# A gated attention and expert layer: gate products one by one beside the first wave's attention, sigmoid at the merge

## The reference

```
n = rms_norm(x);  proj = n @ w_in      # fox q|k|v|forget, sb q|k|v, ga, gb (1024 columns each)
y_fox = fox_attention(...) @ w_o_fox;  y_sb = stick_breaking_attention(...) @ w_o_sb
merged = sigmoid(ga) * y_fox + sigmoid(gb) * y_sb
h = x + merged @ w_out
out = h + peer_ffn(rms_norm(h))        # 8 heads x 16 experts per row, each a row of expert_u and expert_v
```

## Time and profile before

| | us |
|---|---|
| median of 3 runs (3985.39 to 3996.05) | 3988.52 |
| the profiled execution | 3995.0 |
| its span | 3993.0 |
| first gate piece on TensorE (L889) | 158.9 |
| first gather of expert rows (L764) | 538.5 |
| first wave's gate read issued (L737) | 356.6 |

### The profile page before, as it was taken

How to read it: one execution, slowest core, us unless ns; L and a number is a source line. 1 busy time by engine, 2 the same in 40 slices (tenths; PEclk the granted TensorE clock), 3 DMA queues, 4 the chain that set the end, 5 groups by cost and what they waited for, 6 DMA issues and landing times.

```text
span 3993.0 us, 32329 instructions
## 1 busy us (share of the span) xinstructions
PE 3143.7 (79%) x9766; PEld 1628.7 (41%) x9766; DVE 2769.3 (69%) x5660; ACT 1196.2 (30%) x2585; POOL 1392.3 (35%) x1087
## 2 busy tenths in 40 slices
PE   8998957879888697868887779997587878767655
PEld 3344633334436243335445435553262333234222
DVE  2021388678758967767867988886888866567766
ACT  1242111146511111146621146662101444011110
POOL 0000014335323324424333334443334434434553
PEclk9978978878788888978888989988798878878787
DMA  4422269999999969988999989999999888999997
GB/s 157 140 77 107 95 247 381 405 382 412 369 427 379 380 236 406 409 333 354 359 382 380 393 329 403 398 374 368 404 404 398 345 342 356 415 408 384 414 423 323
DMA packets 296027, 1367.21 MB, mean 342 GB/s; under 512 B 36056, under 2 KB 96624, under 8 KB 149392
## 3 DMA queue, kind: packets, MB, share of 16 engines
q0 software_dynamic: 154464, 1116.02, 68.5%
q1 hardware_dynamic: 110480, 222.78, 15.3%
q10 hardware_dynamic: 30912, 26.35, 2.0%
HBM read 1329.52 MB, written 35.10 MB: 342 GB/s over the span
## 4 chain that ended last, share of the span: by engine, by line
PE 40%; DVE 22%; DMA 17%; ACT 8%; issue 6%; SPq 3%; ACTq 2%; POOL 1%; DVEq 0%; POOLq 0%
PE pv L861 12%; DMA uv<-expert_uv,rows_u 9%; DVE uv L1488 9%; PE pb L1049 6%; PE pb L990 5%; SPq L572 3%; DVE held L1511 3%; PE pb L843 3%; PE pb L963 3%; PE pb L814 3%; PE pb L938 3%; PE pv L889 2%; DMA arena<-scratch_c_p 2%; ACTq L97 1%; DMA arena<-scratch_gates 1%
## 5 line engine op out<-in xcount | busy, mean ns | idle before, releaser
L764 POOL DMA_INDIRECT uv<-expert_uv,rows_u x1024 | 1336.5, 1305 | 1994.8 <-PE pv L861 1169.7
L861 PE MATMUL pv<-uv,diag 128*128 128x512 f32 x2344 | 1253.8, 692 | 337.2 <-ACT diag L1193 261.7
L1488 DVE CUSTOM_DVE_ANT_0 uv<-uv,nr 128x1024 f32<-128x1024 f32 x1056 | 1241.9, 1220 | 214.5 <-DMA uv<-expert_uv,rows_u 181.6
L861 PEld LDWEIGHTS pv<-uv,diag 128*128 128x128 f32 x2344 | 508.8, 225 | 985.8 <-issue 906.8
L1049 PE MATMUL pb<-arena 128*128 128x512 f32 (+1 forms) x1248 | 566.4, 613 | 74.2 <-DVE arena L1636 53.1
L1511 DVE SCALAR_TENSOR_TENSOR held<-uv,wgt,held 128x1024 f32<-128x1024 f32 x470 | 604.1, 1285 | 16.9 <-DVE wgt L1499 0.5
L1200 ACT ACTIVATE gel<-dots 128x4 f32<-128x4 f32 x264 | 54.2, 205 | 1720.6 <-DVE dots L1488 1658.0
L1049 PEld LDWEIGHTS pb<-arena 128*128 128x128 f32 (+1 forms) x1248 | 235.7, 192 | 383.2 <-issue 344.4
L814 PE MATMUL pb<-arena 64*128 64x512 f32 (+4 forms) x480 | 227.5, 590 | 124.4 <-DMA arena<-scratch_c_p 46.6
L990 PE MATMUL pb<-arena 128*128 128x256 f32 (+1 forms) x1280 | 260.9, 363 | 2.2 <-ACT arena L1293 2.2
L990 PEld LDWEIGHTS pb<-arena 128*128 128x128 f32 x1280 | 227.9, 194 | 42.2 <-issue 12.9
(11 more groups left out here) (180 smaller groups left out, 2658.0 us busy)
## 6 DMA issues: line engine op xcount, KB each, us to landing
arena<-w_stream SPq DMA_DIRECT2D x80, 1024.0 KB, 9.2
arena<-w_main SPq DMA_DIRECT2D x60, 1024.0 KB, 11.5
uv<-expert_uv,rows_u POOLq DMA_INDIRECT x1024, 12.0
scratch_gates<-arena ACTq DMA_DIRECT2D x32, 256.0 KB, 8.7
arena<-scratch_gates SPq DMA_DIRECT2D x8, 1024.0 KB, 19.6
o<-x SPq DMA_DIRECT2D x14, 512.0 KB, 8.3
arena<-scratch_c_p SPq DMA_DIRECT2D x8, 520.0 KB, 13.2
arena<-x_t SPq DMA_DIRECT2D x8, 512.0 KB, 4.8
```

The costliest lines, as they stand in the source:

```text
L764: pool.indirect_dma_start(out=uv[k % NU][:].rearrange("p a n -> p (a n)"), out_offset=None, in_=io["expert_uv"][:, :], in_offset=bass.Indi ...
L861: mm = nc.tensor.matmul(pv[:, c * BANK:(c + 1) * BANK], diag[n % ND][:], uv[k % NU][:, 1, c * BANK:(c + 1) * BANK], start=n == first, stop ...
L1488: nc.vector.tensor_tensor_reduce(out=u, in0=u, in1=row[:], scale=1.0, scalar=0.0, op0=ALU.mult, op1=ALU.add, accum_out=dots[b % 2][:, k % ...
```

## The change

The gate pieces of the first wave are no longer made as wholes. `gate_run(i)` makes product i % 8 of piece i // 8. The three pieces ahead of the attention are 24 such products in a row, as before. The other nine are 72 products, two in each of the 36 steps from -2 to 33 (`runs_at`): one between the value products and the turns, one behind the scores. A piece so spreads over four steps, and the last one ends in step 33 (before: the block of step 30). ScalarE takes a piece one step after its last product (before: two steps after its block), and the last piece at the start of the merge.

The piece is stored without its sigmoid (`ACT.Copy` with the row's scale), so the two table loads around it are gone within the loop. In the merge of a wave whose first tile is 0 or 8, that is waves 0 and 4, ScalarE applies the sigmoid in place to the gates that were read back, one instruction of 2048 columns for each tile, behind the copies of the turned outputs, and VectorE's gate products wait for it (`gated`). Waves 1 to 3 stay as they are.

```diff
--- before.py
+++ after.py
@@ -294,10 +294,19 @@
     return GATES + j // ABREAST, j % ABREAST
 
 
-def piece_at(s):
-
-    j = ABREAST + (s + 2) // 4
-    return j if (s + 2) % 4 == 0 and j < PIECES else None
+RUNS = 2
+RUNS_OF_PIECE = KD
+
+
+def runs_at(s):
+
+    n = ABREAST * RUNS_OF_PIECE + (s + 2) * RUNS
+    return [i for i in range(n, n + RUNS) if ABREAST * RUNS_OF_PIECE <= i < PIECES * RUNS_OF_PIECE]
+
+
+def pieces_done_at(s):
+
+    return [i // RUNS_OF_PIECE for i in runs_at(s) if i % RUNS_OF_PIECE == RUNS_OF_PIECE - 1]
 
 
 def tile_of(k):
@@ -468,7 +477,7 @@
         turned, turned_out = sem("turned_b"), sem("turned_b_out")
         summed_up, o_out = sem("summed_up"), sem("o_out")
 
-        gates_in = [sem(f"gates_in{i}") for i in range(2)]
+        gates_in, gated = [sem(f"gates_in{i}") for i in range(2)], sem("gated")
         x_in = [sem(f"x_in_m{i}") for i in range(2)]
         g_in = sem("g_in")
         chunk_in = [sem(f"chunk_in{i}") for i in range(NW)]
@@ -876,35 +885,39 @@
                         if b:
                             background(b - 1)
 
-                def gates(j):
-
+                def gate_run(i):
+
+                    j, half, f = i // RUNS_OF_PIECE, i % RUNS_OF_PIECE // 4, i % 4
                     (c, ti), r = piece(j), rows_of(NEW[0][piece(j)[1]])
-                    if j >= 2:
+                    n = chunk_no(0, 2 * c + half)
+                    if j >= 2 and half == 0 and f == 0:
                         pe.wait_ge(staged, proj.staged[(0, *piece(j - 2))])
-                    for half in range(2):
-                        n = chunk_no(0, 2 * c + half)
+                    if f == 0:
                         pe.wait_ge(chunk_in[n % NW], 16 * (n // NW + 1))
-                        w = wring[n % NW].rearrange("p (k n) -> p k n", k=4)
-                        for f in range(4):
-                            mm = nc.tensor.matmul(pv[0:r, j % 2 * BANK:(j % 2 + 1) * BANK], x_turned(ti, half * 4 + f, r), w[:, f, :],
-                                                  start=half == 0 and f == 0, stop=half == 1 and f == 3)
-                        if half:
-                            mm.then_inc(proj_ready, 1)
-                        elif ti == ABREAST - 1:
-                            mm.then_inc(chunk_used, 1)
+                    mm = nc.tensor.matmul(pv[0:r, j % 2 * BANK:(j % 2 + 1) * BANK], x_turned(ti, half * 4 + f, r),
+                                          wring[n % NW].rearrange("p (k n) -> p k n", k=4)[:, f, :],
+                                          start=half == 0 and f == 0, stop=half == 1 and f == 3)
+                    if f == 3 and half:
+                        mm.then_inc(proj_ready, 1)
+                    elif f == 3 and ti == ABREAST - 1:
+                        mm.then_inc(chunk_used, 1)
 
                 def attend(g):
                     n0, units = plan.first[g], plan.end[g] - plan.first[g]
                     for s in range(-2, units + 2):
                         if 2 <= s:
                             values(n0 + s - 2)
+                        if not g:
+                            for i in runs_at(s)[0:1]:
+                                gate_run(i)
                         turns = len(plan.turns[n0 + s - 1]) if 0 < s <= units else 0
                         for i in range(turns):
                             turn(n0 + s - 1, i)
                         if s + 2 < units:
                             scores(n0 + s + 2)
-                        if not g and piece_at(s) is not None:
-                            gates(piece_at(s))
+                        if not g:
+                            for i in runs_at(s)[1:]:
+                                gate_run(i)
                         if 0 <= s < units:
                             beside(("attend", g, s))
 
@@ -1109,8 +1122,8 @@
                         pe.wait_ge(q_out, wave_heads(g))
                     if g == 0:
                         pe.wait_ge(sk_in, 32)
-                        for j in range(ABREAST):
-                            gates(j)
+                        for i in range(ABREAST * RUNS_OF_PIECE):
+                            gate_run(i)
                     if NEW[g]:
                         pe.wait_ge(staged, proj.all_staged[g] if g else proj.staged[0, GATES - 1, ABREAST - 1])
                         pe.wait_ge(col_turned_out, proj.all_turned[g])
@@ -1218,7 +1231,7 @@
                     if c - 2 in QK:
                         act.wait_ge(col_turned, proj.turned[0, c - 2, ti] + 1)
                     act.wait_ge(s_stored[slot], proj.s_stored[0, c - 2, ti])
-                    nc.scalar.activation(stage[slot][0:r], pv[0:r, j % 2 * BANK:(j % 2 + 1) * BANK], ACT.Sigmoid,
+                    nc.scalar.activation(stage[slot][0:r], pv[0:r, j % 2 * BANK:(j % 2 + 1) * BANK], ACT.Copy,
                                          scale=rstd[0:r, ti:ti + 1]).then_inc(staged, 1)
                     act.wait_ge(staged, proj.staged[0, c, ti])
                     act.dma_start(dram["gates"][first_row(t):first_row(t) + r, (c - GATES) * BANK:(c - GATES + 1) * BANK],
@@ -1249,9 +1262,9 @@
                             take_output(n0 + s - 2)
                         if s + 2 < units:
                             magnitudes(n0 + s + 2)
-                        if not g and piece_at(s - 2) is not None:
-                            take_gates(piece_at(s - 2))
-                            nc.scalar.preload_act_table_set("natural_log_exp_and_others")
+                        if not g:
+                            for j in pieces_done_at(s - 1):
+                                take_gates(j)
                         if inside:
                             behind(("attend", g, s))
                             if plan.lots.get(("attend", g, s), ()):
@@ -1260,6 +1273,15 @@
                 def merge(g):
                     tiles = plan.tiles[g]
                     width = sum(query_rows(t) for t in tiles)
+                    if not g:
+                        for j in pieces_done_at(plan.end[0] + 1):
+                            take_gates(j)
+
+                    def sigmoids():
+                        for ti, t in enumerate(tiles):
+                            r = query_rows(t)
+                            act.wait_ge(gates_in[ti], 16 * (g + 1))
+                            nc.scalar.activation(gate[ti][0:r], gate[ti][0:r], ACT.Sigmoid).then_inc(gated, 1)
 
                     def take_outputs():
                         for ti, t in enumerate(tiles):
@@ -1307,6 +1329,8 @@
                         behind(("merge", g, s), 0, early)
                         if step[0] == "outputs":
                             take_outputs()
+                            if tiles[0] in NEW[0]:
+                                sigmoids()
                         elif step[0] == "merged":
                             take_merged()
                         elif step[0] == "norm":
@@ -1656,7 +1680,10 @@
                         cols = slice(c * BANK, (c + 1) * BANK)
                         for ti, t in enumerate(tiles):
                             r = query_rows(t)
-                            dve.wait_ge(gates_in[ti], 16 * (g + 1))
+                            if tiles[0] in NEW[0]:
+                                dve.wait_ge(gated, NEW[0].index(t) + 1)
+                            else:
+                                dve.wait_ge(gates_in[ti], 16 * (g + 1))
                             dve.wait_ge(y_ready, 2 * tiles[0] + c * len(tiles) + ti + 1)
                             for k in range(KINDS):
                                 ins = nc.vector.tensor_tensor(gate[ti][0:r, k, cols], gate[ti][0:r, k, cols], pb[0:r, ti * 2 + k, :], ALU.mult)
```

## The result

The changed kernel takes 3936.7 us (median of 3 runs, 3931.7 to 3943.2) where the kernel before takes 3988.5: a ratio of 0.9868 with a 95% interval of 0.9836 to 0.9899, 52 us faster. The forecast was 3942. Timed again it gave 3938.4 and 0.9868 (0.9851 to 0.9885).

What follows compares the result with a forecast made beforehand. The first wave's unbroken chain of waits, through attention and merge, was taken to bound the time before gathers at 538 us. Attention 48 plus merge 2.5 less last tile 4 gave 46.5 us: 3942 against the median 3988.5, range 3926 to 3967.

Steps and rivals of the forecast that it cites:

- The period: First attention: four steps with eight gate products take 14.6 us plus hand-overs, instead of 20.3.
- hand-overs: First attention: 0.1 us added to each step.
- The round: First attention: scores' start through ScalarE to the next values, 1.3 us, just covered by TensorE's work behind the turns.
- The clock: First attention: TensorE's clock near 1.0 from 180 us to the merge, where it averaged 0.76.
- the rival on the other side: First attention: clock does not stay up; at 0.50 throughout 71 us slower, 4060 us; chance of slower 0.04.
- The tables: First attention: two loads of 1.28 us go from each of nine pieces, already gone from the sum.
- The merge: First wave's merge: turns and first output products at full clock save 2.5 us, both sigmoids hidden.
- The last tile: Wave 4's merge: the added sigmoid costs 4 us, between ends of 2 and 14.
- The rival of 10 us either way: From 700 us on: changed order of gathers and weights shifts the time to 3932 or 3952; taking 10 or more, 0.07.

Runs made afterwards that it cites:

- singles_both_in_front: Changed kernel with both gate products of a step between values and turns, none behind the scores: 3962.4 us, ratio 0.9925 to the kernel before.
- the first experiment: Kernel before with gate pieces kept as whole blocks but stored raw, their sigmoid taken at the merge: 3987.1 us, ratio 0.9999.
- blocks_raw_filled: Whole raw blocks as in the first experiment, plus 21 unread 512-column products in steps without a piece: 3966.5 us, 0.9943 to the kernel before.

## Why the prediction was right

*The period.* 14.6 us and 0.4 of hand-overs were put down; step 2 began at 190.04 us (forecast 190.2) and step 6 at 204.43, so 14.4. Without a piece of tile 8 the periods took 14.4 to 14.6, and the two with one 15.7 (204.43 to 220.12, and the one from 249.12). Step 30 began at 293.81 for 295.2 with its hand-overs, and the outputs were turned at 306.84 for 308. The way, from groups' starts at full clock, was sound. That it came so close is in part luck, for its terms miss in opposite directions: the mask, put at 0.2 us, takes 0.06 or 0.07 from its start to the next product's, a single gate product, put at 0.865, takes 0.91 to 0.96 (227.90 to 228.86, 230.00 to 230.92), no hand-overs show beyond this, and that the pieces of tile 8 are dearer was not foreseen. The round was just covered, and its 1.3 us were right; because of the mask what covers it was overrated, which is why both products in front cost 22 us and not 16 in singles_both_in_front.

*The clock.* It was the condition of the whole forecast, and it held at 1.00. In the kernel before, it fell behind two short steps (those of 245.80 and 248.16 us) and not three. Against the rival on the other side stood that full-width products fill part of every step; the fillers, which are just that, raised the clock of the whole blocks from 0.76 to 0.97.

*The tables.* Right in the sum, since it was made from TensorE's groups and not by adding up savings. But the account of causes that I held at the first experiment gave the loads and part of the clock 22 to 33 us by themselves; alone they gave 5.5 of the attention and nothing measurable in the time. What I had not seen is that removing a wait of ScalarE leaves the narrow short steps, after which the clock falls anyway.

*The merge.* 2.5 us were expected from turns and first output products at full clock, 1.7 came (from 49.6 to 51.3). All of it is in the turns and copies, 4.48 us for 6.17; the clock did not last into the output products (0.82 from 312 to 320 us), which took 29.4 us for 29.6. The gates landed at 317.2 and 319.6, 10.4 and 12.8 us behind P, the end of the attention, where 9 and 11.8 had been taken: the last piece's store took 4.6 us to land and not 1.9, and SyncE waited for it, so that the read was issued at 312.37, 2 us later than put down. The table load did not come on top because it ran before the wait, and a sigmoid took 1.91, not 2.06 us. The first tile's sigmoid was through at 319.11, and 4.6 us were to spare, not 2.5.

*The last tile.* 4 us were put down; the changed kernel lost 4.3 to 4.7 in the stage, while the end shows nothing in one pair of kernels and 8 us in another. If it is nothing there, this is the term that was mis-sized and 4 of the 5 us between the forecast and the result. But these 5 us are within the range of the three runs (3931.7 to 3943.2), and need no cause.

*The stream.* The rival of 10 us either way did not come, but a spread of some 10 us to either side in single profiles (3441.6 to 3461.2 us from the first gather to the end) was real and is why single runs can't settle the small terms.

## What to carry to other kernels

Before pricing a wait on a slow engine, look at TensorE's granted clock behind it: if it is low there, removing the wait alone may give nothing, since TensorE then sets the pace at half speed. Independent full-width products belong into every step of a latency-bound loop, behind the instruction whose result makes the round through the other engines, not in a block; where there are none, even products that nobody reads can pay. And a saving ahead of a stream was worth its full size at the end here, while small costs within a stream that fills the DMA engines may not show there at all.

## What was not expected of the hardware

Added work made a kernel faster: 21 products more, 20.6 us less. With both products in front TensorE idled up to 0.76 us in a step, more than the 0.59 us of a period of the raw blocks, and the clock stayed at 1.00 (98.9 of 112 us busy, the window below), while in the kernel of whole raw blocks it was 0.76 at 105.3 us busy: recorded busy time does not tell whether the clock holds.

```profile
188.00:300.00 112.00, 98.91 (x375) 50.01 (x374) 30.98 (x83) 46.24 (x178) 0.00 (x0) 1.00 0.28 89
```

Single products for the 48 rows of tile 8 are not cheaper than those of 128 rows but dearer: 0.99 us from start to start against 0.91 to 0.96. The values that follow take 0.95 for 0.85 us (x6), the turns 0.05 more, and from the mask to the next product it is 0.16 for 0.06; together this is the 1.3 us by which these periods are longer. In a block of eight, 48 rows cost nearly the same as 128 (6.99 and 6.92 us in blocks_raw_filled). Why is not shown. Here is such a step of the changed kernel:

```profile
212.73 1.06 PE L897 MATMUL pv<-arena 128*48 128x512 f32 x2
213.72 0.55 PE L840 MATMUL pb<-ident,uv 128*128 128x128 f32 x3
...
214.86 0.23 PE L827 MATMUL pb<-masks,ident_b 128*128 128x128 bf16 x1
215.02 1.06 PE L897 MATMUL pv<-arena 128*48 128x512 f32 x2
216.00 1.02 PE L852 MATMUL pb<-uv 128*128 128x64 f32 x6
216.95 1.06 PE L897 MATMUL pv<-arena 128*48 128x512 f32 x2
```
